# Layer 0 of the context before that of the latents: most of the latents' mixer moved into the expert gather

## The reference

```python
# layer 0
f_l, z_l, u_l, dt_l = parts(h_lat)       # one input projection per stream: h @ w_in
f_c, z_c, u_c, dt_c = parts(h_ctx)
y_c, y_l = ssd_bidir(u_c, u_l, dt_c, dt_l, p)   # each direction scans the context first
out = concat([fourier_mix(f), rms_norm_groups(y * silu(z))]) @ w_out
x_lat, x_ctx = x_lat + g1 * out_lat, x_ctx + cg1 * out_ctx
tokens = concat([h2_lat, h2_ctx])
ff = peer(tokens, p)
# peer: per token and head, top 16 of 128x128 product keys
u = jnp.take(p["peer_u"], experts, axis=0)
act = gelu(einsum("thkd,td->thk", u, hb)) * gates
v = jnp.take(p["peer_v"], experts, axis=0)
out = einsum("thk,thkd->td", act, v)
# layer 1: latent attention over context and latents, then peer on the latents alone
```

## Time and profile before

| | |
|---|---|
| median of 3 runs | 4523.26 us (4522.11 to 4526.36) |
| the profiled execution | 4527.93 us |
| its span | 4526.1 us, granted clock 0.831 |
| busy share: PE, DVE, POOL, ACT | 68%, 63%, 33%, 24% |
| moved by DMA | 1488.59 MB, of it 1342.26 MB by the expert gathers |
| first gather of layer 0 issued, last dot ended | 782.4, 2788.6 |
| dots of layer 1 | to 4514 |

### The profile page before, as it was taken

One profiled execution on the slowest core, in us unless ns is written; L12 is line 12 of the kernel. 1 busy time (PEld: TensorE's weight loads), 2 busy tenths in 40 slices (PEclk: granted clock), 3 DMA queues, 4 the chain that ended last, 5 costly groups with the idle time before them and its releaser, 6 DMA issues. The chain is left out here.

```text
span 4526.1 us, 38384 instructions
## 1 busy us (share of the span) xinstructions
PE 3097.1 (68%) x12512; PEld 1370.6 (30%) x12512; DVE 2871.1 (63%) x6909; ACT 1085.6 (24%) x2958; POOL 1491.7 (33%) x1384
## 2 busy tenths in 40 slices
PE   7999979555665565655566565999766665555555
PEld 3645545322222222221222122565422222111111
DVE  1524745777778778775555554664788888555554
ACT  2121222222222222221122211463322222111111
POOL 0001300343443443444344442000344444444443
PEclk9999989787887887777788877999888777777777
DMA  4113731999999999999999996101999999999998
GB/s 167 39 38 124 251 127 58 420 420 415 411 418 414 412 416 410 415 414 422 419 420 421 419 421 283 38 1 37 381 419 420 413 414 405 422 422 421 422 421 348
DMA packets 229660, 1488.59 MB, mean 329 GB/s; under 512 B 25932, under 2 KB 31532, under 8 KB 59220
## 3 DMA queue, kind: packets, MB, share of 16 engines
q0 software_dynamic: 184320, 1342.26, 71.7%
q1 hardware_dynamic: 43764, 139.82, 8.5%
q10 hardware_dynamic: 1376, 4.06, 0.2%
HBM read 1483.76 MB, written 2.28 MB: 328 GB/s over the span
## 5 line engine op out<-in xcount | busy, mean ns | idle before, releaser
L1671 PE MATMUL banks<-arena 128*64 128x512 f32 x5120 | 1604.2, 787 | 1322.3 <-ACT arena L1812 1245.2
L1531 POOL DMA_INDIRECT arena<-experts,arena x1280 | 1419.8, 1109 | 2484.1 <-PE banks L1671 1601.0
L1947 DVE CUSTOM_DVE_ANT_0 arena<-arena 128x1024 f32<-128x1024 f32 x1280 | 1544.1, 1224 | 931.2 <-DMA arena<-experts,arena 912.0
L1671 PEld LDWEIGHTS banks<-arena 128*64 128x64 f32 x5120 | 445.8, 180 | 2389.7 <-ACT arena L1812 1398.1
L1804 ACT ACTIVATE arena<-arena 128x4 f32<-128x4 f32 x320 | 66.1, 206 | 2017.2 <-DVE arena L1947 1993.2
L1812 ACT ACTIVATE arena<-arena 128x64 f32<-128x64 f32 x1280 | 339.4, 335 | 28.3 <-DVE arena L1935 0.4
L1594 PE MATMUL banks<-arena 128*128 128x128 f32 (+2 forms) x1280 | 296.3, 386 | 4.7 <-DMA arena<-wq 2.9
L1594 PEld LDWEIGHTS banks<-arena 128*128 128x128 f32 x1280 | 205.5, 194 | 90.1 <-issue 22.1
L427 PE MATMUL banks<-arena 128*128 128x512 f32 (+1 forms) x640 | 210.3, 488 | 1.8 <-PEq L201 1.8
L1545 PE MATMUL banks<-arena 128*128 128x512 f32 x416 | 183.9, 599 | 2.3 <-PEq L891 1.5
L427 PEld LDWEIGHTS banks<-arena 128*128 128x128 f32 x640 | 121.2, 191 | 87.3 <-issue 79.7
(11 more groups left out here) (240 smaller groups left out, 3133.5 us busy)
## 6 DMA issues: line engine op xcount, KB each, us to landing
arena<-l_w_ada SPq DMA_DIRECT2D x48, 1024.0 KB, 4.9
arena<-wq SPq DMA_DIRECT2D x80, 512.0 KB
arena<-experts,arena POOLq DMA_INDIRECT x1280
arena<-l_w_in SPq DMA_DIRECT2D x7, 2048.0 KB, 8.9
arena<-l_w_out SPq DMA_DIRECT2D x4, 1536.0 KB, 12.7
arena<-keys SPq DMA_DIRECT2D x40, 128.0 KB
arena<-l_w_o SPq DMA_DIRECT2D x4, 1024.0 KB, 8.4
arena<-gates SPq DMA_DIRECT2D x6, 512.0 KB, 6.5
```

The costliest lines, as they stand in the source:

```text
L1531: pool.indirect_dma_start(slots[u % NS], None, tbl, bass.IndirectOffsetOnAxis(ap=expert[:, c % RING, k:k + 1], axis=0)).then_inc(land[u % ...
L1671: mm = pe.matmul(core["ps"][QS * j:QS * j + QS, c, :], diag[:, g % 2, k, :], v[:, D + c * 512:D + (c + 1) * 512], start=(g % (NB * PH) == ...
L1947: dve.tensor_tensor_reduce(u, u, rep[i // PH % 2][:, k % NQ, :], 1.0, 0.0, ALU.mult, ALU.add, dots[:, k:k + 1]).then_inc(dot["sem"], up(dot))
```

## The change

The context goes ahead. Before the gather, scan, gates, output projection, norms and queries are done for tiles 4 and 5 alone. The scan stage (now `ssd_context_stage`) has 16 steps, with slices 3, 3, 2 to a step from four buffers. The gather of layer 0 takes its tiles in the order 4, 5, 0, 1, 2, 3. At its positions the four engines also do the latents' part: scan step n from position n on (32 steps, the groups of heads outermost, `lat_front`, exponentials, `lat_mask`, `lat_products`, `lat_add`), the gates of head group q from position 10 + 8q, the output projection in halves at positions 38 to 45 and 48 to 55, norms behind it. silu(z) and the latents' Fourier columns are stored to memory and loaded again in the gather, `x` is loaded a second time, `w_out` twice (3 MB each time for the latents, besides the 6 MB ahead of the context's projection). The query groups become (4), (5), (0), (1, 2, 3): 32 events. The tensors of the latents live where slots were: 8 slots up to gather 175, then 6 up to gather 235, then 10, then 11. Halves of choices stand at every second position up to 54, at every position from 58 to 121. In the input projection two weight pieces go to other buffers and are issued earlier, and the dt weights have a place of their own.

```diff
+    plan = [(slot[c], first[c], first[c]["base"]) if c < 2 else (slot[c], ring[slot[c] or 0], 0) for c in range(8)]
+    nth = {2: 1, 3: 1, 4: 2, 6: 2, 7: 3}
...
+    assert NS == 3 * NQ + 1
+    slices_of = lambda n: [(n // 3, k) for k in ((0, 1, 2), (3, 4, 5), (6, 7))[n % 3]] if n < 3 * NQ else []
+    turn_of = lambda n: n // 3 - 1 if n and n % 3 == 0 else None
+    ada_w = [view(core, o, GP) for o in (RO + 3328, RO + 5376, RO + 7424, ZSL_O)]
+    AR = len(ada_w)
...
+                for q, k in slices_of(n):
+                    m = q * KD + k
+                    pe.wait_ge(al[m % AR]["sem"], at(al[m % AR], 16 * (m // AR + 1)))
+                    ada_slice(pe, core, ada_w[m % AR], k, 7).then_inc(am["sem"], up(am))
...
 PEER_MAPS = (
-    {"groups": ((0,), (1, 2), (3, 4, 5)), "halves": 3, "w": RO, "g1": L0 + 15360, "g2": L0 + 17408,
-     "diag": L0 + 18432, "wq": L0 + 20480, "sc": L0 + 22528, "keys": L0 + 24064,
-     "rep": (L0 + 3072, L0 + 5120), "ht": HO,
-     "slots": [RO + n * ROWS for n in range(6)] + [L0] + [L0 + 7168 + n * ROWS for n in range(5)]},
+    {"order": (4, 5, 0, 1, 2, 3), "pre": 2, "groups": ((4,), (5,), (0,), (1, 2, 3)), "w": RO,
+     "g1": LAT_Y, "g2": HO + 9728, "diag": HO + 8192, "wq": XSC_O, "sc": ZSC_O, "keys": ZSC_O + 1536,
+     "rep": (HO + 4096, HO + 6144), "ht": HO + 11520, "slots": [RO + n * ROWS for n in range(8)]
+     + [XSL_O, XSL_O + ROWS, LAT_W, LAT_W + ROWS, LAT_XN]},
...
+EARLY = 2
+FIRST_LAT, LAT_CHOICE = 16, 58
+LAT_STEPS = 4 * 2 * TL
+LAT_FEW, LAT_MANY, LAT_ALL = 4 * 44, 4 * 59, 4 * 59 + 40
+LAT_GATE = tuple(10 + 8 * q for q in range(SG))
+LAT_OUT = (38, 40, 42, 44, 48, 50, 52, 54)
+LAT_ROWS = (60, 61)
...
+    def chosen(c, part):
+
+        if layer == 1:
+            return 2 * (c - EARLY) + part
+        return 4 * (c - EARLY) + 2 * part if c < FIRST_LAT else LAT_CHOICE + 2 * (c - FIRST_LAT) + part
...
+    for u in range(steps * TOPK):
+        if layer == 1:
+            n = u % 12
+        elif u < LAT_FEW:
+            n = u % 8
+        elif u < LAT_MANY:
+            n = (u - LAT_FEW) % 6
+        elif u < LAT_ALL:
+            n = (8, 9, 10, 11, 0, 1, 2, 3, 4, 5)[(u - LAT_MANY) % 10]
+        else:
+            n = (12, 8, 9, 10, 11, 0, 1, 2, 3, 4, 5)[(u - LAT_ALL) % 11]
...
+                if n == 4:
+                    sp.wait_ge(lbk["sem"], at(lbk, LAT_STEPS))
+                    lat_weights(0)
+                if n == 5:
+                    sp.wait_ge(lac["sem"], at(lac, 5 * LAT_STEPS))
+                    sp.wait_ge(lxo["sem"], at(lxo, 2 * LAT_STEPS))
+                    sp.dma_start(x[:, 0:TL, :], d["x"].rearrange("(t p) n -> p t n", p=P)
+                                 ).then_inc(lxl["sem"], up(lxl, 16))
+                    lat_gates(0)
+                if n == 6:
+                    sp.wait_ge(ltr["sem"], at(ltr, 2 * SG))
+                    sp.dma_start(fl, d["fourier"]).then_inc(lfl["sem"], up(lfl, 16))
+                if n == 7:
+                    sp.wait_ge(omm["sem"], at(omm, 2 * pre + TL))
+                    lat_weights(1)
...
+            def lat_inputs(n):
+                q, r, t = lat_step(n)
+                c = r * HEADS + q * HG
+                if n:
+                    pool.wait_ge(lbk["sem"], at(lbk, n))
+                pool.tensor_tensor(per(XD), per(xs[:, q, t, :]), bcast(DT[:, t, c:c + HG], HD),
+                                   ALU.mult).then_inc(lxo["sem"], up(lxo))
+                pool.wait_ge(lxo["sem"], lxo["total"])
+                pool.tensor_tensor(per(XE), per(XD), bcast(TOE[:, t, c:c + HG], HD),
+                                   ALU.mult).then_inc(lxo["sem"], up(lxo))
+
...
+                    if layer == 0 and u >= 16 and u % 4 == 0 and u // 4 - 4 < LAT_STEPS:
+                        lat_inputs(u // 4 - 4)
+                    if before[u] is not None:
+                        pool.wait_ge(free["sem"], at(free, before[u] + 1))
+                    elif layer == 1:
+                        pool.wait_ge(omm["sem"], at(omm, 2 * pre if u >= 8 else 0))
+                    elif u < 8:
+                        pool.wait_ge(omm["sem"], at(omm, 2 * pre))
+                        pool.wait_ge(oad["sem"], at(oad, 2 * pre))
...
+            def lat_front(n):
+
+                if n >= 1:
+                    pe.wait_ge(leo["sem"], at(leo, n))
+                if n >= 2:
+                    pe.wait_ge(lmo["sem"], at(lmo, n - 1))
+                if n >= 3:
+                    pe.wait_ge(lac["sem"], at(lac, 5 * (n - 2)))
...
+            def lat_products(n):
+                q, r, t = lat_step(n)
+                pe.wait_ge(lmo["sem"], at(lmo, n + 1))
+                pe.wait_ge(lxo["sem"], at(lxo, 2 * n + 2))
+                if n:
+                    pe.wait_ge(lac["sem"], at(lac, 5 * n))
+                M = decay[n % 2]
+                for h in range(HG):
+                    pe.matmul(core["ps"][:, 4, h * HD:(h + 1) * HD], M[:, h * P:(h + 1) * P],
+                              XD[:, h * HD:(h + 1) * HD], start=True, stop=True)
+                pe.matmul(core["ps"][:, 4, GW:2 * GW], bct[:, SG + q, t * P:(t + 1) * P],
+                          HS[:, r, q * GW:(q + 1) * GW], start=True, stop=True)
+                pe.matmul(core["ps"][:, 5, P:P + GW], br[:, t, q * SN:(q + 1) * SN], XE,
+                          start=True, stop=True).then_inc(lbk["sem"], up(lbk))
...
+            def latents(g):
+                if 2 <= g < LAT_STEPS + 2:
+                    lat_products(g - 2)
+                for q in range(SG):
+                    for j in range(2):
+                        if g == LAT_GATE[q] + 2 + j:
+                            lat_gate_turn(q, j)
+                if g < LAT_STEPS:
+                    lat_front(g)
...
+            def lat_mask(n):
+                M = decay[n % 2].rearrange("p (h l) -> p h l", l=P)
+                o = 3 * P * (n % 2)
+                dve.wait_ge(leo["sem"], at(leo, n + 1))
+                dve.wait_ge(lfr["sem"], at(lfr, min(n + 2, LAT_STEPS)))
+                if n:
+                    dve.wait_ge(lbk["sem"], at(lbk, n))
+                dve.tensor_tensor(M, M, core["ps"][:, 5, o:o + P].unsqueeze(1).to_broadcast([P, HG, P]),
+                                  ALU.mult).then_inc(lmo["sem"], up(lmo))
...
+                dve.wait_ge(lbk["sem"], at(lbk, n + 1))
+                dve.wait_ge(lfr["sem"], at(lfr, min(n + 3, LAT_STEPS)))
...
+            def latents_first(g):
+
+                if g == 0:
+                    lat_skip(0)
+                if 2 <= g < LAT_STEPS + 2:
+                    lat_mask(g - 2)
+                if 3 <= g < LAT_STEPS + 3:
+                    lat_add(g - 3)
+                for m_ in range(2 * TL):
+                    if g == LAT_OUT[m_] + 2:
+                        lat_out(m_)
```

More of the change, by code:

```diff
@@ L318 @@
 DT_O = RO + 2 * SLOT + 4 * SEG
-SPLIT_O = MISC
+SPLITC_O = MISC
 SPLITS = 3
@@ L922, in _ @@
         def _(act):
-            for t in range(TT):
+            for t in range(TC):
                 act.wait_ge(gt["sem"], at(gt, t + 1))
@@ L1297, in peer_block @@
     m = PEER_MAPS[layer]
-    groups = m["groups"]
-    tiles = sum(len(g) for g in groups)
+    groups, T, pre = m["groups"], m["order"], m["pre"]
+    tiles = len(T)
+    place = {t: o for o, t in enumerate(T)}
     steps = tiles * PH
@@ L1488, in _ @@
                     stored += 1
+                while layer == 0 and begun < len(LAT_LOADS) and LAT_LOADS[begun] <= query_at.get(e - 1, -1):
+                    lat_load(begun)
+                    begun += 1
                 sp.wait_ge(qmm["sem"], at(qmm, 2 * e - 1))
@@ new lines, in lat_project @@
+            def lat_project(m, part):
+                c, t = divmod(m, TL)
+                if part == 0:
+                    pe.wait_ge(lwl["sem"], at(lwl, 32 * c + 32))
+                    pe.wait_ge(lgo["sem"], at(lgo, 2 * SG))
+                    if m:
+                        pe.wait_ge(oad["sem"], at(oad, 2 * pre + m))
+                else:
+                    pe.wait_ge(lfl["sem"], at(lfl, 16))
+                bank = core["ps"][:, 7, :]
+                for n in range(K // 2 * part, K // 2 * (part + 1)):
+                    k = (n + GROUPS) % K
+                    a = fl[:, k * LAT + t * P:k * LAT + (t + 1) * P] if k < GROUPS else ms[:, k - GROUPS, t * P:(t + 1) * P]
+                    i = pe.matmul(bank, a, lw[:, k, :], start=(n == 0), stop=(n == K - 1))
+                if part:
+                    i.then_inc(omm["sem"], up(omm))
@@ L1644, in _ @@
+            for t in range(EARLY + 4):
+                if t < pre:
                     project(t, 0)
@@ L1657, in _ @@
                         spread_rows(0, j)
-                if 2 <= t < tiles:
+                if 2 <= t < EARLY + 2:
                     spread_choice(t - 2)
+                if t == 3 and layer == 0:
+                    for j in range(NQ):
+                        spread_rows(1, j)
             for g in range(POS):
@@ L1784, in _ @@
```

(4 more changed lines are left out.)

724 lines of the change are left out of this document (485 added, 239 removed).

## The result

The changed kernel takes 4587.5 us (median of 4 runs, 4579.34 to 4592.5) against 4524.7 us before (4 runs). The ratio is 1.0138, 95% interval 1.012 to 1.0155: slower by 63 us. The forecast was 4510 in a range of 4450 to 4590, so the time lies just inside the range and on the other side of the kernel before.

What follows compares the result with a forecast made beforehand. DMA was taken to bound the layer-0 gather, PE the scan and prologue ahead. 178 us saved ahead less 165 paid in the gather gave -13: 4515 profiled, median 4510 us, range 4450 to 4590.

Steps and rivals of the forecast that it cites:

- What is saved ahead of the gather: Stages before the first gather: input projection -5, scan -76, gates -15, prologue -82, together 178 us less.
- The free first choice: Prologue: the first choice, 8.8 us, formerly under other tiles' projection, may stand free; saving taken as 82, not 88.
- Positions 3 to 36: Layer-0 gather, eight slots and a scan step each: 12.2 us a position against 10.86, +45 us (+15 to +95).
- The chain: Gather, slot reuse: last dot, PE's products, new issue, landing, dot; with eight slots position g+2 follows g by S + 18.6.
- one in four: Gather, positions 3 to 36: share of positions whose choice the softmax waits for, with S of 10.
- S: Gather: time from a position's last dot to PE's products; 1.5 us, about 7 where the softmax waits for the choice.
- Positions 45 to 58: Layer-0 gather with six slots: 222 us where 146 stood, +76 (45 to 95), called the largest cost and the surest.
- S + 12.9: Six-slot stretch: time by which position g+1 follows g, taken between S + 13.6 and S + 10.9 at full clock.
- rival 2: Gather: ring hardly binds, PE at full clock, slots land in 5 us; net -97, median 4426; chance 0.13.
- Positions 37 to 44, 59 to 75, 76 to 121: Later gather stretches: +20 for loads between gathers, +12 for query weights and choices, +12 for a choice at every position.
- Rival 1: Gather, positions 3 to 36: PE and DVE in lockstep over mask and scores; net +51, median 4574; chance 0.33.
- Rival 3: Gather: POOL products and DVE dots hold each other up, about 35 us extra; net +22, median 4545; chance 0.08.

Runs made afterwards that it cites:

- the first experiment: The kernel before, with only the change's table of slots in its layer-0 gather (8, 6, 10, then 11 slots): 4748.3 us beside 4518.4.
- ring_late: The kernel before with the change's table of slots and the softmax of a choice moved behind the diagonals: 4636.8 us.
- no_scan: The changed kernel with the latents' 32 scan steps in the gather left out: 4562.5 us.
- no_scan_late: The changed kernel without the latents' scan steps in the gather and with the softmax behind the diagonals: 4504.4 us.

## Why the prediction was right or wrong

**What is saved ahead of the gather: right**, 181.0 for 178. Input projection and Fourier stage -9.8 (forecast -5, outside its 0 to -6), scan -68.6 (-76; 118 us at 377 GB/s with DMA as the bound, where I took 110), gates -14.4 (-15), prologue -88.2 (-82). That the sum is nearer than its terms is luck: the scan gave 7 us less than forecast, the prologue 6 more, the stages ahead 5 more. The free first choice did happen, as PE's wait shows:

```profile
600.32 0.62 PE L1756 MATMUL banks<-arena 128*64 128x16 f32 x8 [6.55 <-DVE arena L2235]
```

PE is idle for 11.0 us of the prologue where it was idle for 1.2, but its work shrank by 98.0 us (154.4 to 56.4), more than the 88 of the eight halves that I had counted.

**Positions 3 to 36: the step that failed.** Forecast 12.2 us, measured 13.5. The chain's terms were right where they stood alone: 1.5 us to PE's start, 3.95 to the issue, and in a drained ring 5.5 us from issue to dot at the median (5.2 to 6.3 in the six-slot stretch of the first experiment; I took 6.0). Three things were not. First I counted the wait of a choice for the one chain of positions it stands in, "one in four", as if the even and the odd positions were chains of their own. But ACT and PE carry out their queues in order: PE's block of 6 us starts late and the next position's block, gathers and mask all come behind it. In the changed kernel PE's start plus the issue come 15 us after the last dot at positions with a first half of a choice, and still 10 us after it at the position behind, where 5.4 was counted. The mean of S over the stretch was 3.6 us by the forecast and 5.6 in the trace; it falls to 2.6 when the softmax moves, and the time by 38 to 43 us. Second, I put the further bytes of this stretch at nothing: 340 GB/s for 459.6 us is 156.3 MB, where 416 GB/s for 367.2 us was 152.8, an estimated 8 us at 415 GB/s, if the transfer sets the pace. Third, by my chain the eight slots cost nothing where S is 1.5, (1.5 + 18.6) / 2 = 10.05 us being less than the 10.86 of the transfer; `ring_late`, with the softmax behind, took 11.6. Where those 27 us come from stays open. Of the 85 us that the ring costs in the kernel before, 58 are the softmax's place and 27 the ring (452.6, 394.4, 367.2).

**Positions 45 to 58: right in kind, too small.** I had called it the largest cost and the surest; it is 100 us for 76. The step that failed here is the size of the constant: S + 12.9 was S + 14.7 on the mean of the fourteen positions (S + 14.3 in the first experiment). The landing took the 6.0 us that I counted. But the fourth dot follows the third by 3.7 us and not by 2.48, and from PE's start to the issue it is 3.8 us, the lower level of the clock at nearly every block, where I had taken a middle. Even that middle was off: with my own landing of 6.0 the chain at full clock is 2.2 + 6.0 + 2.48 + 1.2 = 11.9, and the S + 10.9 written there belongs to rival 2's landing of 5. 14 positions by 1.8 are 25 us. Longer waits at the three choices (10.0, 6.9 and 9.1 us for 7 each) add 5, and the 4 us that I had put on top for `w_out` lie within these terms: 26 us in all, from 222 to 248.

**Positions 37 to 44, 59 to 75, 76 to 121**: 23.9, 17.0 and 10.2 for 20, 12 and 12; right in kind, by bytes from 59 on (DMA share 1.00).

**Rival 1: its numbers, not its cause.** It gave 4574, 13.6 us for positions 3 to 36 and +90 for the six-slot stretch; the chip gave 4587.5, 13.5 and +100. From these alone it would stand as shown. Its wait is in the profile, on the groups by line of the changed kernel in positions 3 to 36:

```profile
L2324 DVE TENSOR_TENSOR arena<-arena,banks 128x512 f32<-128x512 f32 x32 | 21.9, 684 | 77.7 <-PE banks L1839 65.1 <-issue 10.4 <-PE banks L1855 2.1
```

But the ring without any scan loses as much, and leaving the scan out returns 27 us; with the softmax behind the diagonals 6 to 12. The two waits overlap, since both hang on the same late block of PE: with the choice's wait alone a position takes 12.7 us, with the mask's alone 12.2 to 12.4, with neither 12.1, with both 13.5. The softmax ahead of the diagonals was in my rows as S of 7; I priced it and did not ask whether it had to be there.

**Rival 2 was wrong, and its premise came true in part.** The mean clock did rise with scan steps between the blocks: 0.83 in positions 3 to 36, against 0.72 with the steps left out (`no_scan`) and 0.80 before. The Trainium skill's "TensorE: Matmul & The Clock Gate", section "HAM oscillation — how this bites in real kernels", says that PE falls back in each wait between short pieces of work; the direction of the first two numbers agrees. But the blocks that free the slots did not run at full clock: they take 5.0 us on the mean (170.7 us in 34 positions) where they took 4.5 before (154.2), and 5.6 in `no_scan`. And the clock did not decide: `no_scan`, with the slower blocks, was the faster kernel, and so was `no_scan_late` (0.76, 410.1 us) beside the changed kernel with the same softmax (0.86, 416.2). Both leave work out, so this does not show what the clock alone is worth.

**Rival 3 did not happen.** The POOL products in the gather, by line:

```profile
L1685 POOL TENSOR_TENSOR arena<-arena 128x256 f32<-128x256 f32 x31 | 23.7, 766 | 2.4
L1682 POOL TENSOR_TENSOR arena<-arena 128x256 f32<-128x256 f32 x31 | 22.0, 711 | 12.2 <-PE banks L1855 10.4 <-issue 1.4
```

766 ns for the second, which took 810 in the scan stage. The dots in positions 3 to 36 take 1235 ns on the mean, 1224 in `no_scan`, which is 1.5 us in all; the two additions with both inputs in the arena take 443 and 461 ns, where one took 700 in the scan stage and those with an input in a bank take 408 to 415. The Trainium skill's "SBUF — State Buffer", section "Who interferes with whom", says that a VectorE instruction with two SBUF inputs contends with a GpSimd instruction that reads SBUF. The trace agrees at most in small: the rival wanted 35 us, and these excesses are under 5.

## What to carry to other kernels

Before you shorten a ring of buffers, follow one slot round: last use, release, issue, landing, first use. Each wait in that loop which the longer ring hid will be paid, and on in-order queues it is paid by the positions behind it too, not only by its own. Ask of every wait in the loop whether the instruction behind it needs it: here a softmax for experts of much later positions stood ahead of the diagonals, was worth nothing that one run could show with twelve slots, 111 us with eight and six, and 70 us in the changed kernel.

When a rival's number comes out, test its mechanism all the same. Two waits that hang on the same late block each look like the whole cost in the profile, and taking one away returns a part only.

## What the hardware showed that I had not expected

Gathers of 1.05 MB follow one another at 2.48 us in a full queue. In the six-slot stretch the fourth dot of a position follows the third by 3.7 us on the mean of fourteen positions (3.3 to 4.1, kernel with the short ring) though its gather was issued 1.2 to 2.2 us behind, while the next gathers follow at once. That they share the queue with it is what the order of issues suggests; I did not test it. A short ring thus loses twice: in the wait for its issue, and in the slower landing.
